# In each block of split weights, products with the low part come last and alone wait for GpSimd

## What is computed

```python
def _swiglu(x, w1, w3, w2):
    return (jax.nn.silu(x @ w1) * (x @ w3)) @ w2

for l in range(DEPTH):                      # first stack
    x = _layer_norm(a * x + 0.5 * _swiglu(x, ffn1_w1[l], ffn1_w3[l], ffn1_w2[l]), ln1_g[l], ln1_b[l])
    mix = _token_mixing(x, w_in[l], ...)
    x = _layer_norm(a * x + mix, ln2_g[l], ln2_b[l])
    x = _layer_norm(a * x + _cross_attention(x, mem, ...), ln3_g[l], ln3_b[l])
    x = _layer_norm(a * x + 0.5 * _swiglu(x, ffn2_w1[l], ffn2_w3[l], ffn2_w2[l]), ln4_g[l], ln4_b[l])
```

## Time and profile before

| | |
|---|---|
| median of 3 runs | 3354.95 us (3353.59 to 3355.32) |
| the profiled execution | 3356.97 us, its span 3355.2 us |
| TensorE busy | 2895.5 us, 86% (21913 matmuls) |
| GpSimd busy | 2011.4 us, 60% |
| VectorE / ScalarE busy | 1463.4 us, 44% / 1414.2 us, 42% |
| one subtraction on GpSimd (L310) x836 | 2410 ns |
| one rounding on ScalarE (L790) x836 | 1058 ns |
| mean granted TensorE clock | 0.916 |

### The profile page before, as it was taken

How to read it: one execution, slowest core, us unless ns; L and a number is a source line. 1 busy time by engine, 2 the same in 40 slices (tenths; PEclk the granted TensorE clock), 3 DMA queues, 4 the chain that set the end, 5 groups by cost and what they waited for, 6 DMA issues and landing times.

```text
span 3355.2 us, 58623 instructions
## 1 busy us (share of the span) xinstructions
PE 2895.5 (86%) x21913; PEld 2754.8 (82%) x21920; DVE 1463.4 (44%) x2236; ACT 1414.2 (42%) x2028; POOL 2011.4 (60%) x844
## 2 busy tenths in 40 slices
PE   7989689878999989689878999995699799955996
PEld 7989578777998988678767988994699799944996
DVE  4550424535445441325625555433445554133554
ACT  3444144444444444244444444444444544424444
POOL 6868035454886867035554866873488588712883
PEclk9999589989999999589989999996899899967998
DMA  5545023332554555023333544542255355411551
GB/s 206 181 161 188 16 79 126 113 117 91 182 182 144 182 169 166 19 88 118 120 115 101 181 157 138 181 157 75 92 187 182 114 184 185 157 44 54 188 182 63
DMA packets 122397, 451.74 MB, mean 135 GB/s; under 512 B 13586, under 2 KB 13586, under 8 KB 121364
## 3 DMA queue, kind: packets, MB, share of 16 engines
q1 hardware_dynamic: 120960, 441.43, 39.7%
q10 hardware_dynamic: 1300, 8.39, 0.7%
HBM read 448.72 MB, written 1.05 MB: 134 GB/s over the span
## 4 chain that ended last, share of the span: by engine, by line
PE 35%; POOL 30%; issue 25%; DVE 6%; ACT 2%; POOLq 0%; DVEq 0%; ACTq 0%
POOL wl L310 30%; PE R L344 8%; PE R L347 7%; PE R L348 7%; PE Y L344 2%; PE Y L348 2%; PE Y L347 2%; PE R L449 1%; DVE M L1445 1%; DVE W L1276 1%; PE Y L727 0%; PE Y L492 0%; PE Y L478 0%; PE R L544 0%; PE R L550 0%
## 5 line engine op out<-in xcount | busy, mean ns | idle before, releaser
L310 POOL TENSOR_TENSOR wl<-raw,wh 128x1024 fp32r<-128x1024 f32 x836 | 2010.6, 2410 | 1315.7 <-ACT wh L790 1302.6
L344 PE MATMUL R<-XH,wh 128*128 128x256 f32 x4296 | 1228.0, 286 | 16.5 <-DVE XL L1464 10.9
L347 PE MATMUL R<-XL,wh 128*128 128x256 f32 x4296 | 1220.2, 284 | 0.0
L348 PE MATMUL R<-XH,wl 128*128 128x256 f32 x4296 | 1220.0, 284 | 0.0
L790 ACT ACTIVATE wh<-raw 128x1024 fp32r<-128x1024 f32 x836 | 883.4, 1058 | 790.3 <-PE R L344 474.1
L344 PEld LDWEIGHTS R<-XH,wh 128*128 128x128 f32 x4296 | 829.3, 193 | 29.6 <-issue 26.2
L347 PEld LDWEIGHTS R<-XL,wh 128*128 128x128 f32 x4296 | 829.4, 193 | 0.6
L348 PEld LDWEIGHTS R<-XH,wl 128*128 128x128 f32 x4296 | 829.2, 193 | 0.0
L1215 DVE TENSOR_TENSOR BL<-W,BH 128x256 fp32r<-128x256 f32 x176 | 436.3, 2479 | 6.1
L344 PE MATMUL Y<-BH,wh 128*128 128x256 f32 x1408 | 398.5, 283 | 0.0
L347 PE MATMUL Y<-BL,wh 128*128 128x256 f32 x1408 | 398.5, 283 | 0.0
(11 more groups left out here) (324 smaller groups left out, 2918.7 us busy)
## 6 DMA issues: line engine op xcount, KB each, us to landing
raw<-in_stream SPq DMA_DIRECT2D x836, 512.0 KB, 3.3
G<-in_wcmp ACTq DMA_DIRECT2D x2, 2048.0 KB, 7.6
G<-in_mem ACTq DMA_DIRECT2D x2, 1024.0 KB, 4.7
TB<-in_table SPq DMA_DIRECT2D x1, 1312.0 KB, 6.2
X<-in_x SPq DMA_DIRECT2D x1, 1024.0 KB, 8.5
out_dram<-X ACTq DMA_DIRECT2D x1, 1024.0 KB, 3.9
WS<-in_mix_w ACTq DMA_DIRECT2D x2, 256.0 KB
G<-in_p ACTq DMA_DIRECT2D x2, 256.0 KB, 2.6
```

Source lines behind the costliest of these rows:

```text
L310: pool.tensor_tensor(wl[:, s, :], raw[:, r, :], wh[:, s, :].bitcast(F32), ALU.subtract).then_inc(lo_done, 1)
L344: i = pe.matmul(o, wh[w], hi, start=start, stop=False, skip_group_check=True)
L347: pe.matmul(o, wh[w], lo, start=False, stop=False, skip_group_check=True)
L348: i = pe.matmul(o, wl[w], hi, start=False, stop=stop, skip_group_check=True)
```

## The change

`weights` waits for `hi_done`, ScalarE's rounding, and a new `lows` waits for `lo_done`. In every helper the two products with `wh` run first, for all tiles of the block (for the first chunk of it, where the block has several), then comes `lows`, then the products with `wl`. In `together` all slices of all blocks run with `wh` first; behind the last slice come the products with `wl`, block by block, and `block_begun` for the second and third block moves with them. The number of products and their operands are the same. The cuts marked "..." are the single blocks at L578 and L688, which are changed in the same way.

```diff
             def weights():
                 n = t.n["block"]
-                pe.wait_ge(lo_done, t.up("block"))
+                pe.wait_ge(hi_done, t.up("block"))
                 return n % SPLIT

-            def three(o, w, hi, lo, start, stop, begins=False, end=None):
+            def lows(back=0):
+
+                pe.wait_ge(lo_done, t.value("block") - back)
+
+            def two(o, w, hi, lo, start, begins=False):

                 i = pe.matmul(o, wh[w], hi, start=start, stop=False, skip_group_check=True)
                 if begins:
                     i.then_inc(block_begun, 1)
                 pe.matmul(o, wh[w], lo, start=False, stop=False, skip_group_check=True)
+
+            def third(o, w, hi, stop, end=None):
+
                 i = pe.matmul(o, wl[w], hi, start=False, stop=stop, skip_group_check=True)
                 if end is not None:
                     i.then_inc(end, 1)
+                return i

             def dense(hi, lo, k_tiles=DC, ready=None):
                 s = weights()
                 for j in range(8 // k_tiles):
                     o = claim()
+                    w = lambda k: (slice(None), s, slice((j * k_tiles + k) * P, (j * k_tiles + k) * P + P))
                     for k in range(k_tiles):
                         if ready is not None and j == 0:
                             ready(k)
-                        a = (j * k_tiles + k) * P
-                        three(o[:, 0:T], (slice(None), s, slice(a, a + P)), hi[:, k, :], lo[:, k, :], k == 0,
-                              k == k_tiles - 1, begins=j == 0 and k == 0, end=chunk_ready if k == k_tiles - 1 else None)
+                        two(o[:, 0:T], w(k), hi[:, k, :], lo[:, k, :], k == 0, begins=j == 0 and k == 0)
+                    if j == 0:
+                        lows()
+                    for k in range(k_tiles):
+                        third(o[:, 0:T], w(k), hi[:, k, :], k == k_tiles - 1, end=chunk_ready if k == k_tiles - 1 else None)

             def together(n, hi, lo, ready):
                 for k in range(DC):
                     ready(k)
                     for j, (s, o) in enumerate(zip(slots, outs)):
-                        w = (slice(None), s, slice(k * P, k * P + P))
-                        i = pe.matmul(o[:, 0:T], wh[w], hi[:, k, :], start=k == 0, stop=False, skip_group_check=True)
-                        if k == 0 and j == 0:
+                        two(o[:, 0:T], (slice(None), s, slice(k * P, k * P + P)), hi[:, k, :], lo[:, k, :], k == 0,
+                            begins=k == 0 and j == 0)
+                for j, (s, o) in enumerate(zip(slots, outs)):
+                    lows(n - 1 - j)
+                    for k in range(DC):
+                        i = third(o[:, 0:T], (slice(None), s, slice(k * P, k * P + P)), hi[:, k, :], k == DC - 1,
+                                  end=chunk_ready if k == DC - 1 else None)
+                        if k == 0 and j > 0:
                             i.then_inc(block_begun, 1)
-                        i = pe.matmul(o[:, 0:T], wh[w], lo[:, k, :], start=False, stop=False, skip_group_check=True)
-                        if k == DC - 1 and j > 0:
-                            i.then_inc(block_begun, 1)
-                        i = pe.matmul(o[:, 0:T], wl[w], hi[:, k, :], start=False, stop=k == DC - 1, skip_group_check=True)
-                        if k == DC - 1:
-                            i.then_inc(chunk_ready, 1)
...
                     for c in range(DC):
-                        three(Y[:, c // 2, (c % 2) * T:(c % 2) * T + T], (slice(None), s, slice(c * P, c * P + P)),
-                              HH[:, f % 2, :], HL[:, f % 2, :], False, False, begins=c == 0,
-                              end=end if c % 2 == 1 else None)
+                        two(o(c), w(c), HH[:, f % 2, :], HL[:, f % 2, :], False, begins=c == 0)
+                    lows()
+                    for c in range(DC):
+                        third(o(c), w(c), HH[:, f % 2, :], False, end=end if c % 2 == 1 else None)
...
```

More of the change, by code:

```diff
@@ L388, in tokens_major @@
                     s = weights()
+                    sl = lambda kk: (slice(None), s, slice(kk * 512, kk * 512 + 512))
+                    part = lambda x, k, tt: x[:, k, tt * P:tt * P + P]
                     for kk in range(per):
@@ L391, in tokens_major @@
                         for tt in range(TT):
[L392 to L395, removed]
+                            i = pe.matmul(o[tt], part(hi, k, tt), wh[sl(kk)], start=k == 0, stop=False, skip_group_check=True)
                             if kk == 0 and tt == 0:
                                 i.then_inc(block_begun, 1)
-                            pe.matmul(o[tt], l, wh[sl], start=False, stop=False, skip_group_check=True)
-                            i = pe.matmul(o[tt], h, wl[sl], start=False, stop=last, skip_group_check=True)
-                            if last:
+                            pe.matmul(o[tt], part(lo, k, tt), wh[sl(kk)], start=False, stop=False, skip_group_check=True)
+                    lows()
+                    for kk in range(per):
+                        k = b * per + kk
+                        for tt in range(TT):
+                            i = pe.matmul(o[tt], part(hi, k, tt), wl[sl(kk)], start=False, stop=k == tiles - 1,
+                                          skip_group_check=True)
+                            if k == tiles - 1:
                                 i.then_inc(chunk_ready, 1)
@@ L427, in down @@
                     s = weights()
+                    w = lambda c: (slice(None), s, slice(c * P, c * P + P))
+                    o = lambda c: Y[:, c // 2, (c % 2) * T:(c % 2) * T + T]
                     for c in range(DC):
-                        three(Y[:, c // 2, (c % 2) * T:(c % 2) * T + T], (slice(None), s, slice(c * P, c * P + P)),
-                              HH[:, f % 2, :], HL[:, f % 2, :], False, False, begins=c == 0,
-                              end=end if c % 2 == 1 else None)
+                        two(o(c), w(c), HH[:, f % 2, :], HL[:, f % 2, :], False, begins=c == 0)
+                    lows()
+                    for c in range(DC):
+                        third(o(c), w(c), HH[:, f % 2, :], False, end=end if c % 2 == 1 else None)
                 together(2, XH, XL, ready)
@@ L579, in mixer @@
                 for j in range(4):
-                    three(claim()[:, 0:T], (slice(None), s, slice(j * P, j * P + P)), BH[:, 2, :], BL[:, 2, :], True, True,
-                          begins=j == 0, end=chunk_ready)
+                    o, w = claim()[:, 0:T], (slice(None), s, slice(j * P, j * P + P))
+                    two(o, w, BH[:, 2, :], BL[:, 2, :], True, begins=j == 0)
+                    if j == 0:
+                        lows()
+                    third(o, w, BH[:, 2, :], True, end=chunk_ready)
                 for tt in range(TT):
@@ L689, in gla @@
                 for j in range(8):
-                    three(claim()[:, 0:T], (slice(None), s, slice(j * P, j * P + P)), BH[:, j % 4, :], BL[:, j % 4, :], True, True,
-                          begins=j == 0, end=chunk_ready)
+                    o, w = claim()[:, 0:T], (slice(None), s, slice(j * P, j * P + P))
+                    two(o, w, BH[:, j % 4, :], BL[:, j % 4, :], True, begins=j == 0)
+                    if j == 0:
+                        lows()
+                    third(o, w, BH[:, j % 4, :], True, end=chunk_ready)
                 from_dve()
```

## The result

| | median | runs | span of the profiled run | clock |
|---|---|---|---|---|
| kernel before | 3355.14 us | 3353.59 to 3356.51 (4) | 3355.2 | 0.916 |
| changed kernel | 3375.62 us | 3373.64 to 3376.24 (4) | 3374.4 | 0.911 |

The change costs 20.5 us, a ratio of 1.0060 (95% interval 1.0043 to 1.0078). The prediction was 3369.0 with a range of 3359 to 3382, slower. It did get slower, and the measured time lies in the range; the size was 14.1 for 20.5.

The account below looks back on a forecast made before the run. TensorE's own pace of products was taken as the bound in the long loops, not its waits for GpSimd. Terms -4.0 - 1.0 + 8.7 + 6.6 + 2.8 + 1.0 = +14.1 on 3354.95 gave 3369.0 us, range 3359 to 3382.

Parts of the forecast that it names:

- Steady state: Long loops: TensorE's pace of 0.120 us a product, 2.88 us a block, stays as it is; size 0.
- D: Rival: a faster pace, if fewer switches between high and low tiles save time on each product; about 3339 us, chance 0.06.
- The first half's three-block stages: Block behind `together` in the first half's mixers, twice: wait for GpSimd and slow stretch go; -4.0 us (0 to -4.0).
- The second half's: Block behind the three-block `together` of the second half's mixers, twice: 0.5 us of lost distance each; -1.0 (0 to -1.0).
- Pairs behind layer norms: Two-block `together`, three stages: 12 low-part products put off and a later clock, 2.9 us each; +8.7 (4.3 to 11.1).
- Pairs behind RMS norms: Two-block `together`, four stages: low-part products put off, perhaps a later clock, 1.65 us each; +6.6 (5.2 to 8.0).
- `dense` with `ready`: Mixer's end, twice: 7 or 6 more low-part products behind the last slice; 2.1 and 0.7 us, +2.8 (1.4 to 4.5).
- Ends of `ffn`: Eight ends: DVE's first bank comes 1.44 us later, mostly hidden by TensorE's last block and the table load; +1.0.
- What moves with it: Later `block_begun` for a pair's second block, ScalarE's rounding, SyncE's queue and GpSimd's order: no cost, 0.
- A: Rival: in the stages with gaps the clock rises where it does now; +6.7 to +8 us, about 3362.5, chance 0.20.
- B: Rival: clock late everywhere and part of the delay of DVE's first bank reaches the path; +22 to +32, chance 0.12.
- C: Rival: no change, since stages with work put off lie beside a longer path; about 3357 us, chance 0.10.

## Why the prediction was right

- **The bound.** The chain's 30% for GpSimd was no wait of TensorE. The change took every wait for it away and the kernel became slower. Where `dense` alone was changed, the four places gave 7.6 of gain, near the 7.5 worked out from rows 4 and 6.
- **Steady state, 0.** It held: 2.88 us a block, 0.00 in all eight loops. The rival with another pace (D) is out.
- **The first half's three-block stages, -4.0.** -3.9. The stage ended 12.53 after its first product; the sum said 12.5 (244.6 - 232.1). The slow stretch went, as expected. That it went because the wait did is not shown: it is gone from both stages of the run with 16 products of zeros too, where the waits stayed (1.99 and 1.50), so that of the 2.0 of each stage only 0.5 is safely the change's.
- **The second half's, -1.0.** -2.2 in the changed kernel, but -1.0 with only `dense` changed. The earlier block is 0.5 each. The rest varies with no change in these stages: the kernel with only the pairs changed, where they are as before, shows -0.3 and -0.6. That the stage costs nothing in either order holds only at the low clock: with the clock at 1.00 the new order is 1.5 longer.
- **Pairs behind layer norms, 8.7.** 9.4. The two parts were right as mechanisms: 12 products put off, and the clock. It rose only while the low-part products ran, which the prediction priced at 2.2, yet a stage cost 3.0 to 3.4: in the stage shown it rose at 1034.81, when eleven of the sixteen had started. The 2.9 that was taken was a choice between 2.2 and 3.7, and it was close. The run with zeros in the gaps shows the parts, 1.7 and 1.3 to 1.7. The Trainium skill (TensorE: Matmul & The Clock Gate, section on the second failure mode) says that often repeated short idle times between groups of matmuls make the clock swing between its two levels. These stages agree in part: the run that entered them at full clock lost it in them, but once in a stage, without swinging back before the low-part products ran; and in the kernel before, with 0.39 us idle ahead of a slice, it stayed at 1.00.
- **Pairs behind RMS norms, 6.6.** 5.7, which is 1.4 each, the working without a later clock; 1.65 was too much.
- **`dense` with `ready`, 2.8.** 3.3. **Ends of `ffn`, 1.0.** 2.1, 0.3 and 0.23 each, so the sign named for them, equal within 0.2, did not come. The cover by TensorE's last block was nearly exact, and the term left out that the sums then run at DVE's pace.
- **What moves with it, 0.** Nearly: the waits for blocks stayed away, but DVE's rounding ran into GpSimd's subtraction in one stage, 0.2.
- **What was missing.** The sum had no term for stages whose work stays the same and whose place moves. It is +4.7 of 19.2 in the profiled execution. The two kernels that only run later show steps of that size in the same stages without any change of their work: summed over these stages, from the first `ffn` on, the delay grows by 4.5 in the changed kernel, by 4.7 with 8 products of zeros and by 1.8 with 16. So it takes no effect of the new order to get 4.7, and part of it may belong to the one trace of the kernel before. That all of it is such steps is argued from them, not shown; +2.8 were left with the pairs in the old order. The prediction's range held it by the room for other cases, not by a term of its own.
- **Luck.** That the named stages sum to within 0.4 is in part luck: the terms were off by +0.7, -0.9, +0.5, +1.1, -1.2 and +0.1, and these cancel.
- **Rivals.** A (the clock rises where it did) held behind RMS norms and failed behind layer norms. B (+22 to +32) was right on the late clock behind layer norms and wrong on DVE's first bank, which reached the path with 2.1 of 11.5; the measured total came to its edge (+22) by what was missing and not by its mechanism. C (hidden) is out: the next block followed at once in all twelve stages, and the delay stayed.

## What to carry to other kernels

Putting work behind a wait pays only where that wait binds; ask of each stage what hides the work now. Here four places waited for GpSimd, while seven two-block stages and two mixer ends waited for slices from VectorE and had most of their low-part products hidden in those waits; one order for both lost more than it gained, and the new order in `dense` alone won. An edit that thins TensorE's work in a stage with gaps also puts the clock at risk, and that can double its price, as it did in three stages here.

## What the runs showed of the hardware

- Adding work made a kernel faster: 14 products of zeros in each of three stages took 1.3 to 1.7 us from each, by the granted clock (in the first of them 0.50 from 809.53 to 823.18 without the zeros, and 0.96 to 1.00 from 812.94 on with them).
- With a slice each 1.37 us, 4 products of 0.120 us to a slice let the clock fall from 1.00 to 0.50 in three stages; with 6 to a slice it stayed at 1.00 in the same stages of the kernel before, once it had risen.
- The same work from cross attention ran at a mean clock of 0.88, 0.64 or 0.80 and took 3.2 and 1.2 us more than in the kernel before, after an edit 1500 us earlier that adds 0.9 or 1.8. A change under some 3 us in one execution of this kernel says little about a cause; a comparison by stages does.
- One rounding on DVE of 128x256 took 0.29 us when it began just ahead of a subtraction on GpSimd and 2.46 us when it began just behind the start of one.
